# Attention's front in the scan stage, low parts of the dense mixer on VectorE, out_proj's squares and half of w_out inside attention, value products spread over items

## What is computed

```python
def token_mixers(h, w_in, ..., w_out, ctx):
    proj = h @ w_in
    z, xbc, dt_raw, cq, ckv, k_rope = jnp.split(proj, [s1, s2, s3, s4, s5], axis=-1)
    ...                                          # convolution and the two SSD scans give y_ssd
    y_ssd = rms_norm(y_ssd.reshape(b, length, SSD_WIDTH), ssd_norm)
    q = (rms_norm(cq, q_norm) @ w_uq).reshape(b, length, MLA_HEADS, MLA_NOPE_DIM + MLA_ROPE_DIM)
    ckv_n = rms_norm(ckv, kv_norm)
    ...                                          # latent tokens: rotate q_rope and k_rope, prepend the cache
    kv = (ckv_all @ w_ukv).reshape(b, n_keys, MLA_HEADS, MLA_NOPE_DIM + MLA_V_DIM)
    o = blocked_attention(q_full, k_full, v).reshape(b, length, MLA_WIDTH)
    o = rms_norm(o, mla_norm)
    y = jnp.concatenate([y_ssd, o], axis=-1) @ w_out

def swiglu(u, w_gate, w_up, w_down):             # layer 0, 2816 hidden columns
    return (jax.nn.silu(u @ w_gate) * (u @ w_up)) @ w_down
```

## Time and profile before

| | us |
|---|---|
| three runs | 2295.19, 2285.56, 2292.55; median 2292.55 |
| profiled execution | 2294.19 |
| its span | 2292.4 |
| mean granted clock of PE | 0.929 |
| busy PE, DVE, ACT, POOL | 1998.2, 1325.6, 980.4, 294.0 |
| layer 0: attention starts, out_proj starts | 243.0, 416.3 |

### The profile page before, as it was taken

How to read it: one execution, slowest core, us unless ns; L and a number is a source line. 1 busy time by engine, 2 the same in 40 slices (tenths; PEclk the granted TensorE clock), 3 DMA queues, 4 the chain that set the end, 5 groups by cost and what they waited for, 6 DMA issues and landing times. The chain is left out here.

```text
span 2292.4 us, 33639 instructions
## 1 busy us (share of the span) xinstructions
PE 1998.2 (87%) x11939; PEld 1710.1 (75%) x11939; DVE 1325.6 (58%) x1996; ACT 980.4 (43%) x1540; POOL 294.0 (13%) x128
## 2 busy tenths in 40 slices
PE   5999699586999999995999798685799999999992
PEld 3997445486999999995996445585688888888882
DVE  3817667553222023205827666542688988889885
ACT  4224113424111112105224123330688888888882
POOL 0310000303332333310310000301000000000001
PEclk9999899797999999997999799795899999999996
DMA  6215312202222122201215600203996743727444
GB/s 250 87 48 218 106 55 74 74 1 74 76 80 76 58 80 78 78 13 65 82 74 189 250 1 1 74 1 139 371 410 247 290 186 153 311 77 289 183 155 192
DMA packets 147304, 301.80 MB, mean 132 GB/s; under 512 B 17408, under 2 KB 85888, under 8 KB 144384
## 3 DMA queue, kind: packets, MB, share of 16 engines
q1 hardware_dynamic: 141488, 279.36, 33.2%
q10 hardware_dynamic: 2832, 10.49, 1.2%
q0 software_dynamic: 2880, 10.49, 1.1%
HBM read 358.20 MB, written 28.61 MB: 169 GB/s over the span
## 5 line engine op out<-in xcount | busy, mean ns | idle before, releaser
L1900 DVE TENSOR_TENSOR ex_wl<-ex_raw,ex_wh 128x1024 fp32r<-128x1024 f32 x364 | 431.2, 1221 | 58.7 <-ACT ex_wh L1779 49.1
L1779 ACT ACTIVATE ex_wh<-ex_raw 128x1024 fp32r<-128x1024 f32 x364 | 376.2, 1059 | 67.4 <-PE psum L1837 52.1
L1837 PE MATMUL psum<-ex_wh,ex_he_hi 128*128 128x512 f32 (+1 forms) x624 | 242.5, 389 | 5.0 <-DVE ex_wl L1900 4.9
L1837 PE MATMUL psum<-ex_wl,ex_he_hi 128*128 128x512 f32 (+1 forms) x624 | 233.5, 374 | 0.0
L1837 PE MATMUL psum<-ex_wh,ex_he_lo 128*128 128x512 f32 (+1 forms) x624 | 233.0, 373 | 0.0
L2048 POOL TENSOR_TENSOR ex_wl<-ex_raw,ex_wh 128x1024 fp32r<-128x1024 f32 (+1 forms) x60 | 160.4, 2676 | 337.1 <-ACT ex_wh L2034 337.1
L2034 ACT ACTIVATE ex_wh<-ex_raw 128x1024 fp32r<-128x1024 f32 (+1 forms) x60 | 68.4, 1142 | 258.9 <-PE psum L2068 244.3
L2068 PE MATMUL psum<-h_hi,ex_wh 128*128 128x320 f32 x704 | 161.4, 311 | 16.4 <-POOL ex_wl L2048 14.9
L2068 PE MATMUL psum<-h_lo,ex_wh 128*128 128x320 f32 x704 | 161.1, 310 | 0.0
L2068 PE MATMUL psum<-h_hi,ex_wl 128*128 128x320 f32 x704 | 160.9, 310 | 0.0
L2096 DVE TENSOR_TENSOR ex_hf<-psum,ex_sg 128x640 f32<-128x640 f32 x22 | 18.1, 825 | 233.9 <-PE psum L2068 233.9
(11 more groups left out here) (377 smaller groups left out, 4426.2 us busy)
## 6 DMA issues: line engine op xcount, KB each, us to landing
ex_raw<-moe_gate_up SPq DMA_DIRECT2D x286, 512.0 KB
ex_raw<-moe_w_down SPq DMA_DIRECT2D x78, 512.0 KB
x<-moe_w_down SPq DMA_DIRECT2D x65, 512.0 KB
wmod_ssd<-w_mod SPq DMA_DIRECT2D x56, 512.0 KB, 5.9
wmod_at<-w_mod SPq DMA_DIRECT2D x24, 512.0 KB, 4.4
ex_raw<-ffn_w_gate SPq DMA_DIRECT2D x22, 512.0 KB, 3.7
ex_raw<-ffn_w_up SPq DMA_DIRECT2D x22, 512.0 KB, 3.8
ex_raw<-ffn_w_down SPq DMA_DIRECT2D x16, 704.0 KB, 4.6
```

Of the source, the lines that this page charges most:

```text
L1779: act.activation(wh[:, i % RING], raw_of(i), ACT.Copy).then_inc(*hi_done.up(1))
L1837: last = pe.matmul(p.psum[:, 2 + g % 2, 0:width], h[:, k], w[:, i % RING, cols], start=(k == 0 and m == 0), stop=(k == KD - 1 and m == 2))
L1900: dve.tensor_tensor(wl[:, i % RING], raw_of(i), wh[:, i % RING].bitcast(F32), ALU.subtract).then_inc(*lo_done.up(1))
```

## The change

1. The scan stage loads the cached latents, the gain row and the rotary tables, into a part of `qkv_room` that it doesn't use, and makes mean, root and reciprocal for attention's latents.
2. Attention's SP queue begins with w_uq. PE turns the latents of three blocks, waits for w_uq, and turns the rest after the first query product. The key rows are turned after the keys' product. ACT takes the scaling of cq, two of three evictions of it, the turned queries, and the squares of y_ssd.
3. In the items, scores of n + 2 come before the turning of n, the maximum of n + 2 before the copy of n. ACT copies the fifth key block. A pair's value products come one key block per item (the last pair's together). ACT squares o in the last four context items, and root and reciprocal for blocks 0 to 3 stand at the stage's end. SP loads two quarters of w_out during the items.
4. In out_proj POOL makes one cast and DVE all low parts, ACT copies the gate rows, and only the context block's root is left.
5. In the dense mixer DVE makes the low parts, two pieces ahead (POOL has no program there any more), and the first down piece waits for the last hidden column only at its last step.
6. A constant tile (`far`) lives only in the first stage.

Core of the diff:

```diff
@@ scan stage @@
+                sp.dma_start(t["past"], io["cache_ckv"][0, l]).then_inc(*ahead_in.up(16))
+                sp.dma_start(t["kvrow"], io["kv_norm"][l].partition_broadcast(P)).then_inc(*ahead_in.up(16))
+                sp.dma_start(t["cos"], io["rope_cos"].rearrange("(b p) r -> p b r", p=P)).then_inc(*ahead_in.up(16))
+                sp.dma_start(t["sin"], io["rope_sin"].rearrange("(b p) r -> p b r", p=P)).then_inc(*ahead_in.up(16))
...
+                act.wait_ge(*lat_mean.at(1))
+                act.activation(t["rstd"][:], t["stat"][:], ACT.Sqrt).then_inc(*lat_root.up())
...
+                    if b == TB - 1:
+                        dve.wait_ge(*squares.at(2 * TB))
+                        stat = t["stat"]
+                        dve.tensor_scalar(stat[:, 0], stat[:, 0], 1.0 / QR, EPS, ALU.mult, ALU.add)
+                        dve.tensor_scalar(stat[:, 1], stat[:, 1], 1.0 / KVR, EPS, ALU.mult, ALU.add).then_inc(*lat_mean.up())
...
+                dve.wait_ge(*lat_root.at(1))
+                dve.reciprocal(t["rstd"][:], t["rstd"][:])
@@ attention, SP @@
...
+                sp.dma_start(wq[:], io["w_uq"][l].rearrange("(k p) f -> p k f", p=P)).then_inc(*w_in.up(16))
                 sp.wait_ge(*zeroed.at(1))
                 sp.dma_start(krt[:, 0, NOPE:QD], io["cache_krope"][0, l]).then_inc(*cache_in.up(16))
-                sp.dma_start(wq[:], io["w_uq"][l].rearrange("(k p) f -> p k f", p=P)).then_inc(*w_in.up(16))
-                sp.dma_start(wkv[:], io["w_ukv"][l].rearrange("(k p) f -> p k f", p=P)).then_inc(*w_in.up(16))
+                sp.dma_start(wkv[:], io["w_ukv"][l].rearrange("(k p) f -> p k f", p=P)).then_inc(*wkv_in.up(16))
...
+                sp.wait_ge(*o_ps.at(PAIRS - 1))
+                for i in range(2):
+                    load_out(p, sp, l, t, i)
@@ attention, ACT @@
+                def part_squares(part, b, j):
+
+                    act.activation(oT[:], part[:, b], ACT.Square,
+                                   accum_out=t["part_stat"][:, b, j:j + 1]).then_inc(*part_sq.up())
+                    act.wait_ge(*part_sq.at(part_sq.sent))
+
+                def keep_rest(n):
+
+                    g, b, h = items[n]
+                    if g < PAIRS:
+                        act.wait_ge(*pt_ps.at(n + 1))
+                        if g >= 2 and n - 1 in closes:
+                            act.wait_ge(*o_ps.at(g - 1))
+                        act.activation(probT[:, g % 2, h % 2, LB, b * P:(b + 1) * P], p.psum[:, 5, 0:P],
+                                       ACT.Copy).then_inc(*pt5_ev.up())
+                for b in range(TB):
+                    take_turned(b)
...
+                    if n >= 1:
+                        keep_rest(n - 1)
+                    if n in returns:
+                        keep_outputs(returns[n])
+                    if n >= len(items) - LB:
+                        act.wait_ge(*o_ev.at(PAIRS))
+                        part_squares(o, n - (len(items) - LB), 1)
                 keep_outputs(PAIRS)
+                act.wait_ge(*part_mean.at(1))
+                act.activation(t["part_rstd"][:, 0:LB], t["part_stat"][:, 0:LB], ACT.Sqrt).then_inc(*part_root.up())
@@ attention, PE @@
...
+                for b in range(3):
+                    turn_latents(b)
+                pe.wait_ge(*w_in.at(16))
...
+                    if b == 0:
+                        turn_latents(3)
+                        turn_latents(4)
                     if b >= 1:
                         turn_queries(pe, b - 1)
                 turn_queries(pe, TB - 1)
 
+                pe.wait_ge(*wkv_in.at(16))
...
                         scores(n + 2)
-                    if n - 1 in closes:
-                        outputs(closes[n - 1], n - 1)
-                    if n - 3 in closes:
-                        turn_outputs(closes[n - 3])
+                    turn_probs(n)
+                    for g, k in products_at.get(n, ()):
+                        pair_outputs(g, k)
+                    if n in returns:
+                        turn_outputs(returns[n])
@@ attention, DVE @@
+                    if n + 2 < len(items):
+                        largest(n + 2)
                     dve.wait_ge(*pt_ps.at(n + 1))
                     if g >= 2 and n - 1 in closes:
                         dve.wait_ge(*o_ps.at(g - 1))
                     if g < PAIRS:
                         home = probT[:, g % 2, h % 2, :, b * P:(b + 1) * P]
-                        dve.tensor_copy(home[:, 0:LB], p.psum[:, 4].rearrange("p (k q) -> p k q", k=LB))
-                        last = dve.tensor_copy(home[:, LB], p.psum[:, 5, 0:P])
+                        last = dve.tensor_copy(home[:, 0:LB], p.psum[:, 4].rearrange("p (k q) -> p k q", k=LB))
...
+                    if n in returns:
+                        take_group(returns[n])
+                dve.wait_ge(*part_sq.at(TB + LB))
+                stat = t["part_stat"][:, 0:LB]
+                dve.tensor_scalar(stat, stat, 1.0 / SSDW, EPS, ALU.mult, ALU.add).then_inc(*part_mean.up())
+                dve.wait_ge(*part_root.at(1))
+                dve.reciprocal(t["part_rstd"][:, 0:LB], t["part_rstd"][:, 0:LB])
@@ out_proj @@
+                load_out(p, sp, l, t, 2)
+                sp.wait_ge(*lo_done.at(1))
+                load_out(p, sp, l, t, 3)
 
             @block.gpsimd
             def _(pool):
-                pool.wait_ge(*landed[0].at(16))
-                pool.tensor_copy(w_hi[:, 0], raw[:, 0]).then_inc(*hi_done.up())
-                for i in range(4):
-                    pool.wait_ge(*hi_done.at(i + 1))
-                    pool.tensor_tensor(w_lo[:, i], raw[:, i % 2], w_hi[:, i].bitcast(F32),
-                                       ALU.subtract).then_inc(*lo_done.up())
+                pool.wait_ge(*landed[0].at(0))
+                pool.tensor_copy(w_hi[:, 0], raw(0)).then_inc(*hi_done.up())
...
+                split_hi(1)
+                act.wait_ge(*gr_ps.at(1))
+                for s in range(2):
+                    last = act.activation(rows[:, s].rearrange("p (a c) -> p a c", a=2), p.psum[:, 4 + 2 * s:6 + 2 * s], ACT.Copy)
+                last.then_inc(*gr_ev.up())
+                split_hi(2)
+                scale_parts(2)
+                split_hi(3)
+                scale_parts(3)
+                act.wait_ge(*mean.at(1))
+                act.activation(rstd[:, LB], stat[:, LB], ACT.Sqrt).then_inc(*root.up())
+                act.wait_ge(*rs.at(1))
+                scale_parts(LB)
...
+                def split_lo(i):
+
+                    dve.wait_ge(*hi_done.at(i + 1))
+                    dve.tensor_tensor(w_lo[:, i], raw(i), w_hi[:, i].bitcast(F32), ALU.subtract).then_inc(*lo_done.up())
+                dve.wait_ge(*landed[0].at(0))
+                dve.wait_ge(*landed[1].at(0))
...
+                split_lo(0)
                 take_turned(0)
+                dve.wait_ge(*sq.at(1))
+                dve.tensor_scalar(stat[:, LB], stat[:, LB], 1.0 / SSDW, EPS, ALU.mult, ALU.add).then_inc(*mean.up())
+                split_lo(1)
+                for i in range(2, 4):
+                    dve.wait_ge(*landed[i].at(16))
+                    split_lo(i)
+                dve.wait_ge(*gr_ev.at(1))
@@ dense mixer @@
-                            pe.wait_ge(hid_ready, (e + 1) * FT)
+                            pe.wait_ge(hid_ready, (e + 1) * FT - 1)
                         steps = KD if i < G_PIECES else FT
                         mh, ml = (hi, lo) if i < G_PIECES else (hh, hl)
                         for k in range(steps):
+                            if i == G_PIECES and k == FT - 1:
+                                pe.wait_ge(hid_ready, (e + 1) * FT)
...
+                    def low_part(i):
+                        dve.wait_ge(hi_done, e * PIECES + i + 1)
+                        dve.tensor_tensor(wl[:, SLOT[i], 0:size(i)], raw[:, i % 2, 0:size(i)],
+                                          wh[:, SLOT[i], 0:size(i)].bitcast(F32), ALU.subtract).then_inc(lo_done, 1)
+                    for i in range(AHEAD):
+                        low_part(i)
                     for i in range(PIECES):
+                        if i + AHEAD < PIECES:
+                            low_part(i + AHEAD)
                         if i < G_PIECES and i % 2 == 0:
```

301 lines of the change are left out of this document (155 added, 146 removed).

## The result

The changed kernel took 2217.84 us, median of four runs (2216.0 to 2219.96), against 2291.95 for the kernel before. The ratio is 0.9682, 95% interval 0.9666 to 0.9698. Forecast were 2221 and a range of 2205 to 2244. The profiled execution's span is 2218.2 us, 74.2 less than before. The page's lines that answer to the first things read before: the span, the engines' busy time, and the slices of PE and its granted clock.

A forecast was written before the change was run, and what follows sets the result against it. PE, near full for most of the span, was taken as the bound, so only its dips count. 2 x (0.9 - 10.5 + 2.4 - 20.5) - 16.4 = -71.8, from 2294.2 to 2222.4, 2221 on the median's basis; range 2205 to 2244.

The forecast's parts named there:

- stage's start + 6.5: Attention front: the query product waits for w_uq and begins 6.5 us into the stage, against 21.0 before.
- the +1.3, +1.6 and +1.1 behind it: Attention front, us added: two blocks' turns left over +1.3, key turns +1.6, PE's restart at the lower clock +1.1.
- The term -1.0 for the new order: Items: DVE's round shortens to about 1.7 us, PE's work only changes order; -1.0 us per layer (-4 to +4).
- The +2.4 for the squares: Context items: ACT squares o four times, some 0.8 us each, beside exponentials; +2.4 us put there.
- the wait for the root at the stage's end: Items' end: DVE waits for ACT's root, table load 1.28 and activation 0.21, partly beside the last products; +1.0 us.
- Rival (a): Items get slower, turned probabilities waiting for two engines' copies: 0.3 us for each of 64 items, +19, 2240; chance 0.14.
- went by the row, with no drain: End of attention: table load counted at the trace's 1.28 us, without the skill page's further 1.38 us of drain.
- the hit on 22.5: Head of out_proj: DVE carries the path and block 1's products begin 22.5 us after the stage's start, so -20.5.
- The start, forecast at -1.1: Dense mixer's start: wins 1.1 us, 1.22 for the first piece instead of some 2.3.
- +1.0 for the turn: Dense mixer's loop turn: DVE must add the last piece and subtract the next first one; +1.0 us (0.7 to 3.3).
- the collision of DVE and POOL: Dense mixer, first down piece: POOL's subtraction stretches DVE's low part to 3.81 us and PE waits 5.37, once per pass.
- Slower rival (d): Dense mixer: low parts stand behind DVE's wait for the running piece, exposing 2.4 us per piece; 2365, chance 0.02.

The follow-up runs named there:

- f_loads: Changed kernel, but cached latents, gain row and rotary tables load at the start of attention, ahead of w_uq: 2224.78 us, ratio 0.971.
- f_stat: Changed kernel, but mean, root and reciprocal of the latents stand at the start of attention again, operands still loaded in the scan: 2216.96 us, ratio 0.9679.
- i_rest_dve: Changed kernel, but DVE copies the fifth key block again and nobody waits for ACT's copy: 2223.41 us, ratio 0.9709.
- i_row: Changed kernel, but a pair's 20 value products come in a row in one item again: 2214.41 us, ratio 0.9672.
- i_sq_end: Changed kernel, but ACT squares o after the last exponential, not between the last four: 2213.43 us, ratio 0.9667.
- o_pool: Changed kernel, but in out_proj the four low parts of w_out are POOL's again: 2229.22 us, ratio 0.9734.
- d_pool_late: Changed kernel, but the dense mixer's low parts are POOL's again; PE's late wait for the last hidden column stays: 2218.5 us, ratio 0.9687.
- best1: Changed kernel, but ACT squares o behind the last exponential and POOL makes the dense mixer's low parts under the late wait: 2216.0 us, ratio 0.9675.

## Why the prediction was right

**Front, -10.5 forecast, -12.6 measured.** The step "stage's start + 6.5" was 5.4, since w_uq landed 5.4 us after issue; that is half of the difference. The rest is in the +1.3, +1.6 and +1.1 behind it, which together came to 3.0, not 4.0. f_loads shows the loads' part as 2.0 and f_stat the statistics' as some tenths. What remains of the 12.6, the turns under w_uq's landing and ACT's share, was not undone alone, so it is argued from the two traces only.

**Items, +2.4 forecast, +3.8 and +2.0 measured.** The sum was near, its terms were not. The term -1.0 for the new order hides a gain of 2.2 to 3.0 (the fifth copy, i_rest_dve) and a loss of 1.7 (the spread products, i_row), neither of which I had priced. The +2.4 for the squares was twice too much (1.2, i_sq_end). In its place came a term that the forecast didn't have: PE at its lower level in the last 12 us, some 1.2 to 1.4. These four make 1.9 of layer 0's +3.8 and 1.4 of layer 1's +2.0. The rest stays open; the wait for the root at the stage's end, forecast at +1.0, would be in it and was not undone alone. So that the sum came near is in part luck. Rival (a), in which the items get slower by 0.3 each, did not come: ACT's copy paid for itself.

**The table load.** The sum went by the row, with no drain. After the change the load at the end of attention starts at 404.76, right behind an activation that began at 404.15 and took 0.60, and the root starts at 406.05, 1.29 later:

```profile
404.15 0.60 ACT L1073 ACTIVATE at_oT<-psum 128x512 f32<-128x512 f32 x1 [2.50 <-issue]
404.76 1.28 ACT L1143 ACT_TABLE_LOAD   x1
406.05 0.21 ACT L1143 ACTIVATE mx_part_rstd<-mx_part_stat 128x8 f32<-128x8 f32 x1
```

The 1.38 us that "ScalarE: Activation LUTs" of the Trainium skill (What ACT_TABLE_LOAD costs) adds for a drain do not show, neither ahead of the load nor behind it.

**Head of out_proj, -20.5 forecast, -20.8 and -20.4 measured.** DVE's chain came as laid out: low parts of w_out ready at 4.3, 10.7, 14.0 and 17.1 us after the stage's start (forecast 4.5, 11.3, 14.9, 18.2), y's low part for block 0 at 8.4 (8.7), for block 1 at 21.1 (22.3). But DVE did not carry the path to the end, as the forecast had it. PE's last wait in the head was 1.15 us for ACT's copy of the gate rows, at 9.9; from there it ran 12.3 us through block 0's 96 products and eight turns, and reached block 1 at 22.2, 1.1 behind DVE (in layer 1, 0.9 behind). The two chains happen to be of nearly one length, so the hit on 22.5 is part luck, and y's second low part could have come a microsecond later at no cost. In the kernel before the first products started at 28.3 us and block 0 took 14.7, the first part at the lower level: 18.4 of the 20.8 are the earlier start, 2.4 the clock, which the forecast didn't name. That DVE's durations come back once POOL is quiet holds, and o_pool shows it from the other side. What the forecast missed behind it is +0.8 in the later blocks.

**Dense mixer, -16.4 forecast, -13.8 measured.** Both waits of 5.37 went (from start to start, the piece in front took 7.04 in place of 12.58), and the first down pieces took 9.68 instead of 12.31 and 12.33 us: 2.6 each at the clock's lower level, forecast 2.8. Together 16.4, forecast 16.3. Mis-sized were the small terms. The loop's turn was +0.6, but the piece behind it took 8.66 us instead of 7.13, part of it at the lower level of the clock after PE's wait of 2.13. The start, forecast at -1.1, came as -0.4 in the gap and +0.9 in the first piece (9.88 instead of 9.01). The forecast had +1.0 for the turn, with an upper bound of 3.3, and nothing for the clock behind it. In i_sq_end the same wait of the loop's turn was not followed by it (7.14). Windows of PE over the turn in the two kernels:

```profile
752.00:770.00 18.00, 15.87 (x98) 15.76 (x98) 5.54 (x5) 5.16 (x5) 0.00 (x0) 0.91 0.41 118
```

```profile
750.00:768.00 18.00, 16.35 (x111) 16.36 (x112) 6.91 (x8) 6.23 (x6) 0.00 (x0) 1.00 0.41 118
```

And the reason given was half wrong. The prediction named the collision of DVE and POOL as what made the wait, and its end as the gain. The collision made it long, but d_pool_late has the whole gain with the collision in place. The forecast did name the late wait beside it, and so its number held. **What the mixer's edit is worth comes from where PE waits, not from who subtracts.**

**Slower rival (d).** No low part was ever late inside the pieces: PE's idle time in the mixer is one wait of 2.13 us.

## What to carry to other kernels

Where one engine holds up another, it costs what reaches the waiting engine late, and PE's lower clock behind its wait (in o_pool 2.8 and 2.5 us). What no engine waits for costs nothing. So first move the wait to the step that needs the data, and only then move the work: the first was free here and gave all of it. Where a stage starts with a transfer of its weights, issue that transfer first; what the transfer covers (here statistics, root and table load) need not be moved elsewhere, while the small loads that the covered work needed were worth 2 us per layer. When two chains end nearly together, as in out_proj's head, shortening one alone gains at most their difference. An order of small pieces is not a gain by itself: spreading twenty products over five items cost 1.7 us per layer, and with a row of twenty the kernel was faster.

## What the runs showed of the hardware

DVE operations that read and wrote SBUF were held beside POOL's subtraction whatever their size: two elements per partition took 4.55 us, ten 3.89, a 128x640 low part 3.91 in place of 0.82. The small ones ended with POOL's: the ten at 427.72, POOL's subtraction at 427.70. DVE operations that read PSUM were not held: of the turned blocks' evictions (128x128) in the kernel before, 16 began beside such a subtraction and took 0.33 to 0.34 us, the others 0.33 to 0.35.

How PE's clock follows short waits was not the same in every kernel. A wait of 2.13 us at the mixer's loop was followed by a piece of 8.6 to 8.7 us in ten of the eleven kernels that have it, and of 7.14 us in i_sq_end. After a wait of 1.55 or less there (the kernel before, d_pool_late, best1) it was always 7.1. At attention's front, though, a wait of 1.61 was followed by a first query product of 5.83 us, against 4.04 for the next block's. At the end of attention, with waits of 0.4 to 1.8 us, PE fell to the lower level in nearly every layer of the kernels with the new items (1.98 us for 16 context products), but not in layer 0 of f_stat and layer 1 of i_sq_end and best1, and never in the two kernels with the old items (1.09). What tips it is open.
